# Overflow list scattered behind the last row gather, overflow round's first gather and weights fetched early

## The reference

```
g_idx = argmax(x @ w_grp + b_grp)                    # 1 of 4 groups
top_v, top_i = top_k(expert logits in that group, 2) # 2 of 8 experts
gates = softmax(top_v) * softmax(group logits)[g_idx]
h = silu(xb @ w_gate[e]) * (xb @ w_up[e])            # xb: rows sent to expert e
y = h @ w_down[e]                                    # 1024 -> 512 -> 1024
out[token] = sum over its two experts of gate * y
x = LN(alpha * x + out)
```

## Time and profile before

| | us |
|---|---|
| median of 3 timed runs | 2574.53 |
| lowest and highest | 2567.22 and 2579.78 |
| the profiled execution | 2571.53 |
| its span, first to last instruction | 2569.7 |
| PE busy | 2264.0 |
| DVE, ACT, POOL busy | 826.3, 483.7, 380.3 |
| mean granted TensorE clock | 0.934 of full speed |

### The profile page before, as it was taken

One profiled execution on the slowest core, in us unless ns is written; L12 is line 12 of the kernel. 1 busy time (PEld: TensorE's weight loads), 2 busy tenths in 40 slices (PEclk: granted clock), 3 DMA queues, 4 the chain that ended last, 5 costly groups with the idle time before them and its releaser, 6 DMA issues. The chain is left out here.

```text
span 2569.7 us, 38844 instructions
## 1 busy us (share of the span) xinstructions
PE 2264.0 (88%) x15287; PEld 1251.7 (49%) x15287; DVE 826.3 (32%) x1811; ACT 483.7 (19%) x1127; POOL 380.3 (15%) x454
## 2 busy tenths in 40 slices
PE   8999998874999999997879999999659999999950
PEld 4675757552443444443536777775424344444420
DVE  2123324542212122123626566532421221211218
ACT  0030405220101001011333433331200110110101
POOL 0000001233111111111500000004231111111106
PEclk9989999976999999998989999989679999999985
DMA  9022104342899999996210000000439999999935
GB/s 334 1 89 75 38 0 145 126 202 83 348 388 384 384 393 382 384 392 240 81 51 3 4 4 1 30 37 33 191 129 388 390 383 381 389 381 388 357 118 191
DMA packets 98412, 534.29 MB, mean 208 GB/s; under 512 B 22592, under 2 KB 46432, under 8 KB 73376
## 3 DMA queue, kind: packets, MB, share of 16 engines
q1 hardware_dynamic: 80448, 491.27, 49.1%
q0 software_dynamic: 17888, 41.99, 4.6%
HBM read 509.37 MB, written 41.45 MB: 214 GB/s over the span
## 5 line engine op out<-in xcount | busy, mean ns | idle before, releaser
L826 PE MATMUL banks<-ring,arena 128*32 128x256 f32 (+3 forms) x10016 | 1333.4, 463 | 7.6 <-DVE arena L1782 4.2
L826 PEld LDWEIGHTS banks<-ring,arena 128*32 128x32 f32 (+2 forms) x10016 | 536.3, 124 | 740.5 <-issue 606.5
L826 PE MATMUL banks<-ring 128*128 128x256 f32 (+2 forms) x848 | 312.0, 519 | 5.0 <-DMA ring<-in_mem_w_kv 3.1
L1779 DVE TENSOR_TENSOR arena<-arena,banks 128x384 f32<-128x384 f32 x65 | 36.0, 554 | 626.4 <-ACT arena L1358 626.4
L826 PEld LDWEIGHTS banks<-ring 128*128 128x128 f32 (+1 forms) x848 | 158.3, 193 | 110.7 <-issue 94.8
L826 PE MATMUL banks<-arena 128*128 (+3 forms) x1472 | 192.0, 288 | 15.4 <-DMA arena<-in_mem_w_kv 9.7
L826 PEld LDWEIGHTS banks<-arena 128*128 128x128 f32 (+1 forms) x1472 | 186.8, 201 | 30.8 <-issue 23.0
L771 POOL DMA_INDIRECT expert_out<-arena,scatter_idx x64 | 60.8, 951 | 929.1 <-DVE arena L1788 849.7
L1358 ACT ACTIVATE arena<-banks 128x384 f32<-128x384 f32 x65 | 31.9, 491 | 809.5 <-PE banks L826 809.5
L701 POOL COPY q_stage<-arena 64x256 f32 (+1 forms) x80 | 31.5, 394 | 841.3 <-PE banks L826 597.6
L1026 PE MATMUL banks<-ident,arena 96*128 96x96 f32 x520 | 61.5, 266 | 103.1 <-DMA arena<-moe_in,gather_idx 80.0
(11 more groups left out here) (173 smaller groups left out, 1752.9 us busy)
## 6 DMA issues: line engine op xcount, KB each, us to landing
ring<-in_exp_w_gu SPq DMA_DIRECT2D x130, 2048.0 KB, 11.6
ring<-in_exp_w_down SPq DMA_DIRECT2D x65, 2048.0 KB, 18.3
arena<-expert_out SPq DMA_DIRECT2D x32, 512.0 KB, 4.3
ring<-in_x_t SPq DMA_DIRECT2D x6, 2304.0 KB, 15.8
moe_in<-arena POOLq DMA_DIRECT2D x16, 512.0 KB, 3.0
ring<-in_a_w_in SPq DMA_DIRECT2D x6, 1024.0 KB, 17.6
arena<-in_a_w_in SPq DMA_DIRECT2D x4, 1024.0 KB, 13.8
arena<-in_x SPq DMA_DIRECT2D x1, 4096.0 KB, 13.1
```

The costliest lines, as they stand in the source:

```text
L826: return nc.tensor.matmul(out, lhsT, rhs, start=start, stop=stop)
```

## The change

GpSimd's 16 scatters of the overflow list, with the three waits ahead of them, move from behind gather 1 to behind the last row gather, ahead of the scatter of expert 28. SP loads the first `over_idx` in either layer, whatever `n_over` is, once those scatters have landed, right after it issued the last down weights; GpSimd issues the first overflow gather (`over_gather(0)`) before the scatters of experts 29 to 31. In the overflow loop gate/up weights wait for the gate/up products only, the down weights for the down products; the index load and gather for a following round come at the end of each round, so the list has CAP more entries that are out of bounds, and TensorE waits at a round's end for the result copies. The slots of layer 0's overflow weights are permuted. The semaphore that only marks places in a loop becomes one for all engines.

```diff
-        slot_d = [nc.dram_tensor(f"overflow_rows_{l}", [SLOTS, 2], I32).ap() for l in range(DEPTH)]
+        slot_d = [nc.dram_tensor(f"overflow_rows_{l}", [SLOTS + CAP, 2], I32).ap() for l in range(DEPTH)]
...
-        OVER_SLOTS = ((0, 1, 2), (2, 3, 4))
+        OVER_SLOTS = ((0, 2, 1), (2, 3, 4))
...
                 down(NE - 1, 1)
 
                 o = ov[l]
+                sp.wait_ge(o["slots"], 256)
+                if l == 1:
+                    sp.wait_ge(ov[0]["xs"], 16)
+                sp.dma_start(over_idx[0:CAP], slot_d[l][0:CAP]).then_inc(o["idx"], 16)
                 if l == 0:
...
-                    sp.wait_ge(down_ps, NE)
-                else:
-                    sp.wait_ge(down_ps, 2 * NE - 1)
                 sp.wait_ge(over_done, l + 1)
                 n_over = sp.value_load(over_i[0:1, NOVER:NOVER + 1], min_val=0, max_val=NOVER)
                 with sp.If(n_over > 0):
-                    sp.wait_ge(o["slots"], 256)
                     with sp.Fori(0, n_over) as j:
                         e = sp.value_load(over_i[0:1, bass.ds(j, 1)], min_val=0, max_val=NE - 1)
-                        sp.dma_start(over_idx[0:CAP], slot_d[l][bass.ds(j * CAP, CAP)]).then_inc(o["idx"], 16)
-                        for m in range(3):
+                        sp.wait_ge(gu_ps, NE * (l + 1) - (l == 1))
+                        for m in range(2):
                             sp.dma_start(part_rows(OVER_SLOTS[l][m]), part_src(l, m, e)).then_inc(o["w_in"], 16)
+                        sp.wait_ge(down_ps, NE * (l + 1) - (l == 1))
+                        sp.dma_start(part_rows(OVER_SLOTS[l][2]), part_src(l, 2, e)).then_inc(o["w_in"], 16)
                         sp.wait_ge(o["out"], 16 * j + 16)
-                        fence(sp)
+                        sp.dma_start(over_idx[0:CAP], slot_d[l][bass.ds(j * CAP + CAP, CAP)]).then_inc(o["idx"], 16)
...
                 gather(0, n0, 0, first=l == 0)
                 gather(1, n0, 1, first=l == 0)
-                o = ov[l]
-                pool.wait_ge(slots_cleared, 32)
-                pool.wait_ge(infos_in, 16)
-                pool.wait_ge(over_done, l + 1)
-                for t in range(TT):
-                    for k in range(2):
-                        pool.indirect_dma_start(slot_d[l][:, :], bass.IndirectOffsetOnAxis(ap=slots_i[:, t, k:k + 1], axis=0),
-                                                infos[:, t, k, :], None, bounds_check=SLOTS - 1, oob_is_err=False).then_inc(o["slots"], 16)
                 gather(2, n0 + 1, 0)
...
                 gather(NE - 1, n0 + NE // 2 - 1, 1)
+                o = ov[l]
+                pool.wait_ge(slots_cleared, 32)
+                pool.wait_ge(infos_in, 16)
+                pool.wait_ge(over_done, l + 1)
+                for t in range(TT):
+                    for k in range(2):
+                        pool.indirect_dma_start(slot_d[l][:, :], bass.IndirectOffsetOnAxis(ap=slots_i[:, t, k:k + 1], axis=0),
+                                                infos[:, t, k, :], None, bounds_check=SLOTS - 1, oob_is_err=False).then_inc(o["slots"], 16)
                 scatter(NE - 4, n0 + NE // 2 - 2, 0)
+
+                def over_gather(n):
+                    pool.wait_ge(o["idx"], 16 * n + 16)
+                    fence(pool)
+                    pool.indirect_dma_start(xs[0:CAP, 0], None, x1_d[l][:, :],
+                                            bass.IndirectOffsetOnAxis(ap=over_idx[0:CAP, 0:1], axis=0),
+                                            bounds_check=S - 1, oob_is_err=False).then_inc(o["xs"], 16)
+
+                pool.wait_ge(xst_ps, NE * (l + 1) - 1)
+                over_gather(0)
                 for e in range(NE - 3, NE):
                     scatter(e, n0 + e // 2, e % 2)
+                pool.wait_ge(o["xs"], 16)
                 n_over = pool.value_load(over_i[0:1, NOVER:NOVER + 1], min_val=0, max_val=NOVER)
                 with pool.If(n_over > 0):
                     with pool.Fori(0, n_over) as j:
...
                         pool.wait_ge(o["y"], j + 1)
                         fence(pool)
                         pool.indirect_dma_start(y_d[l][:, :], bass.IndirectOffsetOnAxis(ap=over_idx[0:CAP, 1:2], axis=0),
                                                 ys[0:CAP, 0], None, bounds_check=2 * S - 1, oob_is_err=False).then_inc(o["out"], 16)
+                        over_gather(j + 1)
+                        pool.wait_ge(o["xs"], 16 * j + 32)
+                        fence(pool)
...
                         down(part_view(OVER_SLOTS[l][2])).then_inc(o["down"], 1)
+                        pe.wait_ge(o["y"], j + 1)
+                        fence(pe)
```

More of the change, by code:

```diff
@@ L181, in build @@
         zeroed = sem("zeroed")
-        fenced = {e: sem(f"fenced_{n}") for e, n in ((nc.sync.engine, "sp"), (nc.gpsimd.engine, "pool"), (nc.vector.engine, "dve"))}
+        fenced = sem("fenced")
         slots_cleared = sem("slots_cleared")
@@ L299, in fence @@
         def fence(eng):
-            eng.sem_inc(fenced[eng.engine], 1)
+            eng.sem_inc(fenced, 1)
         LAYER_UNITS = [NG * TT + TT, MLA_H * TT + TT]
@@ L799, in experts @@
                     with pool.Fori(0, n_over) as j:
[L800 to L804, removed]
                         pool.wait_ge(o["y"], j + 1)
@@ L2022, in constants @@
         "tri": (np.arange(P)[:, None] < np.arange(P)[None, :]).astype(np.float32),
-        "nowhere": np.full((SLOTS, 2), NOWHERE, np.int32),
+        "nowhere": np.full((SLOTS + CAP, 2), NOWHERE, np.int32),
         "infos": infos,
```

## The result

The changed kernel takes 2503.9 us (median of 4 runs, 2498.5 to 2505.4) against 2574.6 before: a ratio on record of 0.9747, with a 95% interval from 0.9717 to 0.9776, so 58 to 73 us less. (The recorded ratio is not the quotient of the medians; these differ by 70.7 us, inside that interval.) The prediction was 2514, that is 57.6 us less. In three measurements in which the changed kernel ran beside the one before, the ratios were 0.9747, 0.9760 and 0.9773: 65, 62 and 58 us. The profiled execution took 2505.4 us, span 2503.5, which is 66.2 us less than the span before.

A forecast was written before the change was run, and what follows sets the result against it. TensorE, busy 88% of the span, was taken as the bound, so only shortening its waits pays. Holes 50.9 + round 7.1 - end 0.4 = 57.6 us off 2571.5 gives 2514, range 2504 to 2528.

The forecast's parts named there:

- The holes: TensorE's stall for expert 2's rows early in each layer's expert phase goes: 25.5 and 25.4 us saved.
- Rival C: Expert loop bound by the weight stream, head's gain waited for later, only the round's part stays: 2565 us; chance 0.04.
- The scatters behind the last gather: The 16 scatters, 1.28 us each after the last row gather, cost 0, at worst 1 us a layer.
- Rival D: GpSimd's 16 issues crawl beside full DMA engines: slower, deciding at 3.3 us each, 2595 us at 4.0; chance 0.03.
- Rival E: VectorE's work holds GpSimd off at each layer's tail, scatters take at most 1.6 us: 2518.5 us; chance 0.06.
- The index load behind 2 MB: SP's overflow index load stands behind 2 MB of down weights taking 7.9 us; it lands between 2437 and 2446, taken as 2443.
- the late half of the bound: By ring order the index load cannot pass the 2 MB, so it lands late within 2437 to 2446.
- in hand for scatter 29: Scatter 29 lands at 2455.6, 3 us before its buffer is written for expert 31; 1 us lacking at the late bound.
- The round: Overflow round's gather and weights come early in layer 1, its matmuls start at 2468.7 instead of 2475.83: 7.1 us saved.
- both low bounds: Scatter 31's landing at 4.0 us and VectorE's control code at 0: 10 us saved at the overflow round.
- Rival B: Overflow round gives nothing, scatter 31 lands as under load, VectorE's control code costs its upper bound: 2520 us; chance 0.10.
- The end: One more index load by SP before the final loads costs 0.4 us, bounds 0 and 1.7.

The follow-up runs named there:

- double_list: The changed kernel with 32 scatters instead of 16 behind the last gather, the first 16 to a spare list; 2520.4 us, ratio 0.9809.
- scatters_only: The kernel before, with only the 16 scatters moved behind the last row gather; 2509.5 us, ratio 0.9778.

## Why the prediction was right

**The holes.** Forecast 25.5 and 25.4 us, measured from gate_up's end 25.4 and 25.3. gather 2 landed before gate_up of expert 0 ended, the half microsecond behind VectorE's product was there, and TensorE's clock stayed at its high level across the former hole: 1.00 from 605 to 622 and from 634 to 646, where it was 0.80 before. No wait on weights followed in the first experts. Rival C (the loop is bound by its weights and the gain is waited for later) is out: the 28 phases behind took 492.5 and 493.2 us against 493.4 and 493.9.

**The scatters behind the last gather.** Forecast free, and free: the stretch from the last transposes to the last copy is 42.9 us as before. Rival D's condition, 3.3 us per scatter, was far off: 1.28. Rival E would have shown as scatters stretched to 1.6 beside VectorE's work; they stayed at 1.28. What the page SBUF - State Buffer of the Trainium skill tells, a GpSimd DMA of 620 ns that took 3100 beside a VectorE copy, did not occur with these instructions.

**The index load behind 2 MB.** Forecast 7.9 us behind the down weights' issue; it landed 7.5 us after its own, at 2383.5, which is 7.6 behind theirs. That is the late half of the bound, as the Trainium skill's rule of ring order (DMA: Bandwidth & Descriptors, "Queues, rings and completion order") had it; the trace agrees. In double_list the same load was issued some 12 us behind the last 2 MB and landed in 1.7 us. Of the 3 us forecast in hand for scatter 29 there were 4.7, since it landed in 8.5 us and not 9.6; double_list shows them used up.

**The round.** Forecast 7.1, measured 8.9. The step that was mis-sized is scatter 31's landing, taken as 5.0 us and measured as 3.6, below the low bound of 4.0; the scatter also started 0.98 us after the last copy, not 1.3. The control code of VectorE took 0.9, against 1.0 taken. With both low bounds the prediction's own sum gives 2475.83 - 2466.68 = 9.2 us, not the 10 that it names. Rival B (nothing gained, 9.6 us of landing) failed since the weights ahead were through: the last 2 MB, issued at 2392.04, had landed 8.8 us later, at 2400.9, before scatter 31 started.

**The end.** Forecast 0.4 lost; SP's extra index load made 0.5 (from the landing of the round's scatter to the first final load 0.99 us instead of 0.51). The whole stretch behind the round's start grew by 1.8. Another 0.4 are the round's matmuls, 12.38 us at a clock that was low for a part of them, which the prediction kept at 12.05. The other 1 us lies behind the first final load and is there in scatters_only too, which has no extra load; its cause is open.

**The sum.** 50.7 + 8.9 - 0.5 = 59.1 from these steps, against 57.6 forecast. The first pair of profiles shows 66.2; 5.7 of the difference is the attention's clock, the rest about 1 us here and there in stretches that vary as much between executions of one kernel. The time itself fits less well than the steps: the measured median, 2503.9, is 0.1 us below the lower end of the range of 2504 to 2528. The forecast took the profiled 2571.5 as its base and knew nothing of the attention's clock. The two later measurements of the changed kernel gave 2507.8 and 2509.6, inside the range, and 62 and 58 us of gain. That the first one came out at the edge is play between executions as far as the traces show, not a further gain.

## What to carry to other kernels

A queue that issues one after the other makes its least urgent work as urgent as whatever stands behind it: ask of every block in it what is needed next, and put the block behind the last item that anyone waits for. Work out the cover there by the first buffer or index that is queued behind it, since it ends (16 scatters free, 16 more 4 us a layer). When a fetch is hidden, the wait that it covered comes up next, here another engine's wait for a landing; look for it in the program order, since a wait that another one covers is hard to see in the trace of before. Compare two profiles at fixed events before crediting the whole difference to the change.

## What the runs showed of the hardware

The same program spent 5.5 us more or less up to the end of layer 0's attention, with a granted clock of 0.92 or 1.00 from 110 to 200 us, in executions of one kernel. Over 11 profiled executions, whose code up to there is the same, the first row transposes came between 587.3 and 600.2 us.

After the same idle time of 1.85 us the same 96 matmuls took 12.38 us in one execution (clock 0.52 over the first 3.6 us) and 10.68 in another (1.00): whether the clock falls at this gap was not the same from one execution to the next.

A scatter of 96 rows on empty queues landed in 3.6 us, in the full loop in 9.6 (median). A gather of 96 rows was used 4.3 us after its start on empty queues and 6.4 beside 4 MB of weights. An index load of 0.8 KB landed in 7.5 us right behind 2 MB on SP's queue and in 1.7 us without them.
